# A transformer kernel's mixers: decays as products, level matmuls inside the projections, output projection begun early

## The chip, the cores and the metric

One core of one Trainium2 chip runs one program. The metric is the device time in microseconds. The kernel before took 1440.02 us (median of 3 runs, 1439.94 to 1443.43).

## The reference

Two transformer blocks on 256 positions of width 1024, in float32. The change lies in the first block's mixers:

```python
h = rms_norm(x, norm_mix); z = h @ w_in           # 9 splits: a_x a_y | b_q b_f b_i b_g | c_q c_k c_v
# LRU group (a_x, a_y; width 256)
xc = causal_conv4(a_x) + conv_b
r, i = sigmoid(xc @ wa + ba), sigmoid(xc @ wx + bx)      # 64x64 blocks
log_a = -8 * r * softplus(-lam); a = exp(log_a)
u = sqrt(-expm1(2 * log_a)) * (i * xc)
h_t = a_t * h_{t-1} + u_t;  ya = h * gelu(a_y)
# HGRN2 group (4 heads of 64)
log_f = log(lb + (1 - lb) * sigmoid(f)); k = (1 - lb) * sigmoid(-f); qs = silu(q)
# lb = cumsum(softmax(.)) - first = 0 for one layer: exp(log_f) = sigmoid(f) (+ tiny)
att[t, s] = sum_d q[t, d] * k[s, d] * exp(b[t, d] - b[s, d])   for s <= t,  b = cumsum(log_f)
yb = rms_norm(att @ v + carried state) * silu(g)
# attention group (8 heads of 64, causal with a linear bias; one block of 256, so no retrieval)
yc = softmax(q k^T / 8 - slope * distance) v
x = x + concat(rms_norm(ya), yb, rms_norm(yc)) @ w_out
# then MLP relu^2, the second block (gated linear attention, spatial gating, PEER), final norm
```

## The kernel before

Each product with a large weight matrix is done in three float32r matmuls: weights and activations are split into an upper and a lower part, and upper x upper, upper x lower and lower x upper are summed. The weights come as one stream of tiles of 128 x 1024 through a ring of four slots. Per tile, SyncE's queue loads `raw` (L310), ScalarE makes `whi` (`hi`, L511), GpSimd (POOL) `wlo` = raw - whi (`lo`, L406), and TensorE multiplies. ScalarE may fill a slot only when the tile four earlier has been used (`tile_used`).

There are two kinds of tiles. `f_tile` (L817 to L819) gives 128 output features by 256 positions from 24 matmuls of 256 columns; its result is in bank 4 or 5 in turn, and VectorE must copy it out (`in_f`) before the tile after next may start. `m_tile` (L834 to L836) adds one eighth of the contraction to four accumulators in banks 0 to 3, with 12 matmuls of 512 columns.

The order of each engine's work is written out by hand, one program per engine, tied by semaphores. The first block goes:

1. Squares, root and scaling of x, transposes (L864), upper and lower halves of the result (L541, L1203).
2. 16 f tiles: the features of a_x, a_y, q, f and the attention's q and k. VectorE copies them (L1270, L1272) and, after every second one, does an `ada_tile` (L1233, L1235), a piece of the second block's modulation vector: its weights have a second stream of 48 tiles, `ada`, with a ring of four slots of its own. `series` is a short polynomial in 2 columns for softplus(-lam).
3. 8 m tiles (values and gate, `zM`), with the LRU's gates (L888) before the fourth. Beside them VectorE makes the convolution (L1319, L1323), gelu's argument, log f by abs, exp and ln (L1335 to L1354), copies `zM` (L1351), and sums log f along time (L1361). ScalarE has the sigmoids (L570 to L580) and exp and ln (L587, L589).
4. The mixers. The scores of HGRN2 need the decay exp(b[t] - b[s]), which would overflow as exp(b[t]) times exp(-b[s]). The positions of each half of 128 are therefore paired at 7 levels with half-lengths h = 1 to 64: a query in the right half of a block of 2h and a key in the left half meet at the block's middle, with both factors at most one. For each level POOL subtracts (`level_diff`, L451), ScalarE takes exps (`level_dec`, L600, L601), POOL multiplies keys and queries into `hK` and `hQ` (`level_qk`, L462, L463), TensorE forms scores over all 128 x 128 pairs (`level_scores`, L966) and VectorE takes those of this level by a mask into `att` (`level_acc`, L1374). Level 0 is the diagonal, and an eighth step (L954) ties the two halves of 128. Between the levels stands one attention head each: `a_scores` (L914, L915), `a_soft` (L1386, L1389), `head_exp` (L609), `a_turn` (L924), `head_pT` (L1396), `a_values` (L933 to L935). The LRU's parts are at levels 3 and 5 (L1407 to L1417, with the scan in L1415). Then the LRU is transposed (L989), HGRN2's values are formed (L997, L1000), and the norms follow: squares (L526), POOL's root (L425, L427), scalings (L1446 to L1455).
5. y is transposed as a whole (L864, group `y_T`), split (L541, L1203), and 8 m tiles of `w_out` follow (group `wout`). After them come a modulation column group (`ada_columns`, L898) and the MLP's transposes (L864 with `xs`), then the MLP.

## Time and profile before

| | |
|---|---|
| runs | 1440.02 us median (1439.94 to 1443.43) |
| profiled execution | 1442.89 us, span 1441.1 us |
| busy: TensorE, VectorE, ScalarE, POOL | 1382.1, 769.4, 721.9, 1080.5 us |
| mean granted TensorE clock | 0.967 |
| first projection, f tiles; m tiles | 47.63; 25.76 us |
| mixers; output projection | 63.77; 23.80 us |

An engine's busy share says little by itself: TensorE is busy 96% of the span, and in the mixers it is busy too, but at half clock for much of it. The stretches of the first block are to be read apart, with the granted clock beside them. A row of the timeline has start and duration in us, engine, line, operation, operands, and in brackets the idle time before it and what ended it. Matmuls are pipelined: the distance between two starts is what a group costs.

### The profile page before, as it was taken

What the parts mean: (1) busy time and instruction counts of PE and PEld (TensorE: products, weight loads), DVE (VectorE), ACT (ScalarE), POOL (GpSimd) and SP (SyncE); (2) the same over time, 40 slices, a digit from 0 to 9 for tenths busy, and PEclk for the clock granted to TensorE, in tenths of its full rate; (3) what the DMA queues carried; (4) which work ended last, traced back from release to release, by engine and by line L of the source; (5) the groups of instructions that cost most, each with busy time, mean ns of one, the idle gap of its engine ahead of it and who ended that gap; (6) DMA issues with size and microseconds to landing.
All of it is one profiled execution on the core that took longest, in us unless ns stands there. A gap on an engine that the chain in (4) does not pass through costs nothing.

```text
span 1441.1 us, 29039 instructions
## 1 busy us (share of the span) xinstructions
PE 1382.1 (96%) x9746; PEld 1232.9 (86%) x9746; DVE 769.4 (53%) x1612; ACT 721.9 (50%) x1139; POOL 1080.5 (75%) x495
## 2 busy tenths in 40 slices
PE   6997899999899999899999999999999999999997
PEld 6976799999877787799999999999977777788885
DVE  3567433333518734519994156666678888611113
ACT  5364365555445454434556543344445555566664
POOL 7755578888569877686888877777767777788885
PEclk9986899999899999899999999999999999999999
DMA  9711467775444547654555554444444544475552
GB/s 343 282 45 60 156 216 284 274 289 196 176 148 161 171 136 261 205 182 133 188 178 186 179 171 160 159 156 157 155 146 162 172 161 162 161 259 190 190 197 94
DMA packets 72649, 262.99 MB, mean 182 GB/s; under 512 B 8208, under 2 KB 9104, under 8 KB 72224
## 3 DMA queue, kind: packets, MB, share of 16 engines
q1 hardware_dynamic: 72608, 262.46, 53.3%
q8 instruction: 23, 0.38, 0.1%
q14 instruction: 18, 0.15, 0.0%
HBM read 259.81 MB, written 2.62 MB: 182 GB/s over the span
## 4 chain that ended last, share of the span: by engine, by line
PE 85%; DVE 6%; issue 3%; POOL 2%; ACT 2%; DMA 1%; SPq 0%; POOLq 0%; ACTq 0%; DVEq 0%
PE bank L817 14%; PE bank L818 13%; PE bank L819 13%; PE bank L834 13%; PE bank L835 12%; PE bank L836 12%; PE bank L1132 3%; POOL wlo L406 2%; DVE arena L1563 1%; DMA raw<-stream 1%; PE bank L966 1%; DMA arena<-ada 1%; PE bank L898 1%; PE bank L1114 1%; PE bank L864 0%
## 5 line engine op out<-in xcount | busy, mean ns | idle before, releaser
L406 POOL TENSOR_TENSOR wlo<-raw,whi 128x1024 fp32r<-128x1024 f32 x432 | 1042.6, 2426 | 301.3 <-ACT whi L511 297.8
L511 ACT ACTIVATE whi<-raw 128x1024 fp32r<-128x1024 f32 x432 | 453.8, 1052 | 190.6 <-PE bank L836 99.4
L817 PE MATMUL bank<-xh,whi 128*128 128x256 f32 x1600 | 459.9, 287 | 6.9 <-DVE xl L1203 4.4
L818 PE MATMUL bank<-xl,whi 128*128 128x256 f32 x1600 | 453.9, 284 | 0.0
L819 PE MATMUL bank<-xh,wlo 128*128 128x256 f32 x1600 | 453.7, 284 | 0.0
L817 PEld LDWEIGHTS bank<-xh,whi 128*128 128x128 f32 x1600 | 308.3, 193 | 10.5 <-POOL wlo L406 5.0
L818 PEld LDWEIGHTS bank<-xl,whi 128*128 128x128 f32 x1600 | 308.4, 193 | 1.2
L819 PEld LDWEIGHTS bank<-xh,wlo 128*128 128x128 f32 x1600 | 308.1, 193 | 0.0
L834 PE MATMUL bank<-whi,uh 128*128 128x512 f32 x640 | 255.4, 399 | 2.3 <-DVE ul L1757 2.3
L835 PE MATMUL bank<-wlo,uh 128*128 128x512 f32 x640 | 250.4, 391 | 0.0
L836 PE MATMUL bank<-whi,ul 128*128 128x512 f32 x640 | 249.9, 390 | 0.0
L1757 DVE TENSOR_TENSOR ul<-bank,uh 128x256 fp32r<-128x256 f32 x128 | 54.4, 425 | 183.7 <-ACT bank L784 183.7
L836 PEld LDWEIGHTS bank<-whi,ul 128*128 128x128 f32 x640 | 120.5, 188 | 25.4
L834 PEld LDWEIGHTS bank<-whi,uh 128*128 128x128 f32 x640 | 120.8, 189 | 24.4 <-DVE ul L1757 2.4
L757 ACT ACTIVATE arena<-bank 128x256 f32 x128 | 49.3, 385 | 181.0 <-PE bank L819 180.8
L835 PEld LDWEIGHTS bank<-wlo,uh 128*128 128x128 f32 x640 | 120.8, 189 | 21.9
L783 ACT ACTIVATE uh<-arena 128x256 fp32r (+1 forms) x128 | 53.5, 418 | 164.0 <-PE bank L836 160.8
L1742 DVE TENSOR_TENSOR xs<-bank,xs 128x768 bf16<-128x768 f32 x128 | 121.7, 951 | 0.0
L834 PE MATMUL bank<-whi,xh 128*128 128x512 f32 x288 | 116.3, 404 | 5.2 <-POOL wlo L406 2.4
L835 PE MATMUL bank<-wlo,xh 128*128 128x512 f32 x288 | 114.3, 397 | 0.0
L836 PE MATMUL bank<-whi,xl 128*128 128x512 f32 x288 | 113.8, 395 | 0.0
L1750 DVE TENSOR_TENSOR arena<-arena,bank 128x256 f32 (+1 forms) x128 | 53.3, 416 | 67.3 <-PE bank L1132 67.3
(284 smaller groups left out, 1346.4 us busy)
## 6 DMA issues: line engine op xcount, KB each, us to landing
raw<-stream SPq DMA_DIRECT2D x432, 512.0 KB, 3.3
arena<-ada SPq DMA_DIRECT2D x48, 512.0 KB, 4.3
arena<-rows SPq DMA_DIRECT2D x5, 512.0 KB, 7.5
xs<-x SPq DMA_DIRECT2D x2, 512.0 KB, 4.4
arena<-rows SPq DMA_DIRECT2D x1, 1024.0 KB, 4.6
x_spill<-xs SPq DMA_DIRECT2D x1, 1024.0 KB, 6.2
xs<-x_spill SPq DMA_DIRECT2D x1, 1024.0 KB, 5.6
out<-arena SPq DMA_DIRECT2D x2, 512.0 KB, 2.6
```

What stands on the lines that cost most here:

```text
L406: nc.gpsimd.tensor_tensor(wlo[:, slot, :], raw[:, slot, :], whi[:, slot, :].bitcast(F32), ALU.subtract).then_inc(lo_done, 1)
L511: nc.scalar.activation(whi[:, slot, :], raw[:, slot, :], ACT.Copy).then_inc(hi_done, 1)
L783: nc.scalar.activation(uh[:, c % 2, :], src, ACT.Copy)
L817: nc.tensor.matmul(dst, h_, xh[:, k, :], start=(k == 0), stop=False)
L818: nc.tensor.matmul(dst, h_, xl[:, k, :], start=False, stop=False)
L819: last = nc.tensor.matmul(dst, l_, xh[:, k, :], start=False, stop=(k == KC - 1))
L834: nc.tensor.matmul(bank[b][:, :], ah[:, ts], whi[:, slot, cs], start=start, stop=False)
L835: nc.tensor.matmul(bank[b][:, :], ah[:, ts], wlo[:, slot, cs], start=False, stop=False)
L836: last = nc.tensor.matmul(bank[b][:, :], al[:, ts], whi[:, slot, cs], start=False, stop=final)
L1742: ttt(oneA[:, slot], same.unsqueeze(1).to_broadcast([P, 3, 4, HALF]), picks[:, 2:5, ts].unsqueeze(3).to_broadcast([P, 3, 4, HALF]), ALU.mu ...
L1750: ttt(dst, dst, bank[6 + q % 2][:, 0:4 * HALF].rearrange("p (t n) -> p n t", t=4), ALU.mult)\
L1757: ttt(ul[:, c % 2, :], bank[5][:, 0:T], uh[:, c % 2, :].bitcast(F32), ALU.subtract)\
```

## The change

It does the following.

- **Decays as products.** log f, its running sum, and the exps per level are gone. sigmoid(f) and 1 - sigmoid(f) come from one exp, an addition, a reciprocal and a product (q's sigmoid likewise, and f and q are first raised to at least -85). `totals(h)` multiplies neighbours, so that `tot(h)` (banks 6 and 7) holds the product of the decays over each run of h positions, with a copy in SBUF. From level to level `level_up(h)` multiplies the keys of each left half by the product of its right neighbour's run, and the queries of each right half by that of its left one, in place. `hQ`, `hK`, `hdec`, and all of POOL's and ScalarE's level work go.
- **Level matmuls between tiles.** `level_scores(0)` stands after f tile 13, 1 to 7 before m tiles 1 to 7, the cross-half one behind. Levels 6 and 7 form only the blocks that are used; levels 5 to 7 share banks and one masked copy.
- **LRU within the f tiles.** The f tiles are reordered (`F_ORDER`), so that a_x comes first, then f, q, a_y. Convolution, gates (after tile 4), decay, scan and gelu lie between the copies of the f tiles, with intermediate results in banks 0 to 3.
- **Modulation tiles.** The twelve `ada_tile`s of this part move from the f tiles (0 to 7) and the output projection (8 to 11) to levels 2 to 5 (0 to 3) and the output projection (4 to 11); their DMAs in SyncE's queue move along. Column group 1 is formed after the output projection.
- **Mixers.** Only the attention, the HGRN2 values and the norms are left. `head_pT` goes from VectorE to ScalarE, the next scores wait for the raw copy (`a_raw`) and not the minimum, silu(g) is made from tanh.
- **Output projection.** `y_turn(b)` transposes two of the eight column blocks of y at a time: LRU and HGRN2 blocks within heads 5 and 6, the attention's before m tile 3. The first tile takes banks 2, 3, 0, 1.

The diff, cut to its core:

```diff
@@ tables @@
+TOT_AT = {2: 0, 4: 256, 8: 384, 16: 448, 32: 480, 64: 496}
+F_ORDER = [0, 1, 6, 7, 4, 5, 2, 3, 8, 9, 10, 11, 12, 13, 14, 15]
+    if group == "wout":
+        return (("att_y", 1), ("att_y", 2), ("a_pT", 8), ("a_raw", 8))[bank]
...
+        def tot(h):
+            return bank[7][:, :] if h == 1 else bank[6][:, TOT_AT[h]:TOT_AT[h] + 512 // h]
@@ SyncE @@
+            for n in range(R, T_FFN):
+                tile(n % R, n * P, n - R + 1)
+                if n in range(T_IN_M, T_IN_M + R):
+                    ada_tile(n - T_IN_M)
+                if n in range(T_WOUT, T_WOUT + R):
+                    ada_tile(n - T_WOUT + R)
...
@@ POOL: level_diff and level_qk go @@
-            los(R, T_WOUT)
...
+            los(R, T_WOUT + R)
             root(S("squares"), squared("lru"), s_(SS["lru"]), rs("lru"), 1.0 / 256)
+            root(S("hg_ss"), 1, hss, hrs, 1.0 / 64)
             root(S("squares"), squared("att"), s_(SS["att"]), rs("att"), 1.0 / 512)
@@ ScalarE, f tiles @@
+            nc.scalar.activation(hk, zF[:, 6:8, :], ACT.Exp, scale=-1.0).then_inc(S("hk_exp"), 1)
+            upper_of(R + 4, R + 6)
             act.wait_ge(S("lru_gates"), 1)
...
+            upper_of(R + 6, R + 7)
+            act.wait_ge(S("in_f"), 6)
+            nc.scalar.activation(hq, zF[:, 4:6, :], ACT.Exp, scale=-1.0).then_inc(S("hq_exp"), 1)
...
@@ TensorE @@
+            def level_scores(n):
+                pe.wait_ge(S("h_qk"), n + 1)
...
+                first = 4 if n else 2
+                for odd in range(2):
+                    ps = slice(64 * odd, 64 * odd + 64)
+                    for c in range(2):
...
+                        h = P if n < 6 else LEVELS[n - 1]
+                        for tt in range(TT):
+                            dst, at = (2 * tt + c) * P, tt * P
+                            for a in range(0, P, 2 * h):
+                                ks = slice(at + a, at + a + h)
+                                qs = ks if h == P else slice(at + a + h, at + a + 2 * h)
...
+                                last = nc.tensor.matmul(bank[first + odd][a:a + h, to], hk[ps, c, ks], hq[ps, c, qs],
+                                                        start=True, stop=True)
+                    last.then_inc(S("h_sc"), 1)
...
+            m_group(T_IN_M, "in_M", before=lambda k: level_scores(k) if k else None)
+            level_scores(8)
...
+            for h in range(8):
+                a_turn(h)
+                if h + 2 < 8:
+                    a_scores(h + 2)
+                if h == 0:
+                    hg_values()
+                if h:
+                    a_values(h - 1)
+                if h >= 5 and h < 7:
+                    y_turn(h - 5)
+            a_values(7)
+            def att_turn(k):
+                if k == 3:
+                    y_turn(2)
+                    y_turn(3)
+            m_group(T_WOUT, "wout", "y", before=att_turn, first_banks=(2, 3, 0, 1))
@@ VectorE @@
+            def totals(h):
+                even_odd = lambda t_: t_.rearrange("p (a two) -> p a two", two=2)
+                src, copy_ = even_odd(tot(h)), even_odd(tot_copy(h))
+                for dst in (tot(2 * h), tot_copy(2 * h)):
+                    own(ttt(dst.unsqueeze(2), src[:, :, 0:1], copy_[:, :, 1:2], ALU.mult))
...
+            own(tsc(two(bank[1]), hq, 1.0, None, ALU.add)); own.sync()
+            own(nc.vector.reciprocal(bank[1][:, :], bank[1][:, :])); own.sync()
+            ttt(hq, two(bank[1]), zF[:, 4:6, :], ALU.mult).then_inc(S("h_qk"), 1)
...
+            def level_up(h):
...
+                own(ttt(k0, t2[:, :, 1:2].to_broadcast([P, 256 // h, h]), k0, ALU.mult))
+                ttt(q1, t2[:, :, 0:1].to_broadcast([P, 256 // h, h]), q1, ALU.mult).then_inc(S("h_qk"), 1)
...
+            for n in range(1, 8):
+                v.wait_ge(S("h_sc"), 2 * n + 2)
+                v.wait_ge(S("h_qk"), n + 1)
+                level_up(LEVELS[n - 1])
+                if n < 5 or n == 7:
+                    level_acc(n)
+                if 2 <= n < 2 + R:
+                    ada_tile(n - 2)
```

What moves, at three places. First TensorE. Before, behind the last m tile of the first projection (L836), a head's scores, two modulation column groups and the levels (L966) begin:

```order
L836 MATMUL bank<-whi,xl 128x512
L914 MATMUL bank<-arena 128x128 [waits in_m]
L915 MATMUL bank<-arena 128x256
L898 MATMUL bank<-st,arena 128x1 [waits ada_used,ones_set]
L898 MATMUL bank<-st,arena 128x1 x3
L966 MATMUL bank<-arena 128x128 [waits ri_done,hb_done]
L966 MATMUL bank<-arena 128x128 x7
L914 MATMUL bank<-arena 128x128 [waits a_max]
```

Now level 7 (L899) stands between two of those m tiles (L826 to L828), and only the cross-half step (L889) is behind them, ahead of the first scores (L935):

```order
L828 MATMUL bank<-whi,xl 128x512
L899 MATMUL bank<-arena 64x64 [waits h_qk]
L899 MATMUL bank<-arena 64x64 x7
L826 MATMUL bank<-whi,xh 128x512 [waits lo_done]
...
L889 MATMUL bank<-arena 128x128 [waits h_acc,h_qk]
L889 MATMUL bank<-arena 128x128 x3
L935 MATMUL bank<-arena 128x128 [waits in_m]
L936 MATMUL bank<-arena 128x256
```

The eight matmuls of a level have moved in front of a tile, and they wait for `h_qk`, which VectorE gives.

Second VectorE within the f tiles. Before, between the copies of tiles 11 and 12 (L1272, L1270), a modulation tile (L1235, `arena` the weights) and the polynomial in 2 columns:

```order
L1272 TENSOR_SCALAR arena<-bank 128x256 [waits tile_used] x2
L1235 SCALAR_TENSOR_TENSOR bank<-arena,st,bank 128x512 [waits ada_used,ada_full1]
L1235 SCALAR_TENSOR_TENSOR bank<-arena,st,bank 128x512 [waits dve_steps]
L1295 TENSOR_TENSOR bank<-bank,arena 128x2
```

Now, between the copies of tiles 7 (L1285) and 8 (L1283), q's sigmoid, and behind tile 8's the first products of decays (L1324):

```order
L1285 COPY arena<-bank 128x256 [waits tile_used]
L1366 TENSOR_SCALAR bank<-arena 128x512 [waits xc_done,hq_exp]
L1367 RECIPROCAL bank<-bank 128x512 [waits dve_steps]
L1368 TENSOR_TENSOR arena<-bank,arena 128x512 [waits dve_steps]
L1283 TENSOR_SCALAR arena<-bank 128x256 [waits tile_used]
L1324 TENSOR_TENSOR bank<-bank,arena 128x256
```

The copy of tile 8 now stands behind a wait for ScalarE's exp and a reciprocal, and tile 10 waits for that copy.

Third TensorE at the start of the output projection. Before, the last value products of HGRN2 (L997, L1000), then all of y's transposes (L864) and the first m tile:

```order
L997 MATMUL bank<-arena 128x64
L1000 MATMUL bank<-arena 128x64
L864 MATMUL bank<-ident,arena 128x128 [waits unturned]
L864 MATMUL bank<-ident,arena 128x128 x7
L834 MATMUL bank<-whi,xh 128x512 [waits turned_lo,lo_done]
```

Now the second y turn (L987), the last head's turn (L945) and the values of the last two heads (L954 to L956) stand right before it:

```order
L987 MATMUL bank<-ident,arena 128x128 [waits y_ready]
L987 MATMUL bank<-ident,arena 128x128 x3
L945 MATMUL bank<-ident,arena 128x128 [waits a_pT,a_exp]
L945 MATMUL bank<-ident,arena 128x128 x2
L954 MATMUL bank<-arena 128x64 [waits a_pT]
L955 MATMUL bank<-arena 128x64
L956 MATMUL bank<-arena 128x64
L826 MATMUL bank<-whi,xh 128x512 [waits a_pT,lo_done,turned_lo]
```

The first m tile no longer waits for a transpose of the whole y, only for its first two blocks.

## Rows read from the trace of the kernel before

**Rows 1.** Stretches: length, busy time (instructions) by engine, granted clock, DMA share, GB/s.
```profile
14.65:62.28 47.63, 47.63 (x384) 47.63 (x385) 22.80 (x58) 20.02 (x23) 38.73 (x17) 0.96 0.85 315
62.28:88.04 25.76, 24.31 (x114) 18.93 (x112) 19.07 (x29) 16.86 (x21) 12.87 (x6) 1.00 0.49 168
88.04:151.81 63.77, 48.40 (x302) 41.58 (x301) 44.97 (x82) 28.89 (x75) 34.86 (x34) 0.63 0.10 34
151.81:175.61 23.80, 23.80 (x99) 19.56 (x99) 10.15 (x17) 8.57 (x11) 15.93 (x7) 0.92 0.50 176
```
**Rows 2.** Timeline of ScalarE, one upper half in each kind of tile.
```profile
48.08 1.06 ACT L511 ACTIVATE whi<-raw 128x1024 fp32r<-128x1024 f32 x1 [1.82 <-PE bank L819]
...
162.04 1.06 ACT L511 ACTIVATE whi<-raw 128x1024 fp32r<-128x1024 f32 x1 [1.66 <-PE bank L836]
```
**Rows 3.** Waits, 100 to 180: us in total, times, longest.
```profile
DVE xs L1465 <- PE bank L836: 13.2, 1, 13.2
...
PE bank L966 <- DVE arena L1374: 7.6, 2, 5.1
...
PE bank L864 <- DVE arena L1455: 6.3, 1, 6.3
```
**Rows 4.** Stretches as in rows 1, within the mixers and at the output projection's start.
```profile
90.80:104.20 13.40, 13.40 (x79) 11.42 (x79) 7.15 (x17) 7.57 (x24) 10.06 (x11) 0.50 0.00 1
104.20:111.85 7.65, 7.65 (x71) 6.08 (x70) 7.37 (x15) 3.80 (x11) 6.75 (x8) 0.99 0.01 2
...
128.49:141.20 12.71, 12.68 (x67) 11.71 (x67) 6.68 (x14) 7.04 (x16) 6.81 (x6) 0.50 0.26 88
147.47:155.30 7.83, 7.17 (x24) 6.10 (x25) 4.83 (x11) 3.03 (x8) 0.00 (x0) 0.50 0.00 0
```
**Rows 5.** Timeline of TensorE: gates, one head at half clock, one level at full.
```profile
72.08 1.95 PE L888 MATMUL bank<-arena 64*64 64x256 f32 x16 [1.45 <-DVE arena L1323]
...
98.48 0.63 PE L914 MATMUL bank<-arena 64*128 64x128 f32 x2
...
99.89 0.69 PE L933 MATMUL bank<-arena 128*128 128x64 f32 x2
...
101.22 0.85 PE L924 MATMUL bank<-ident,arena 128*128 128x128 f32 x3
102.00 2.08 PE L966 MATMUL bank<-arena 64*128 64x128 f32 x16
...
105.99 1.16 PE L966 MATMUL bank<-arena 64*128 64x128 f32 x16
106.99 0.38 PE L914 MATMUL bank<-arena 64*128 64x128 f32 x2
107.21 0.59 PE L915 MATMUL bank<-arena 64*128 64x256 f32 x2
```
**Rows 6.** VectorE's groups by form, 26 to 62: busy, mean ns, idle before.
```profile
L1235 DVE SCALAR_TENSOR_TENSOR bank<-arena,st,bank 128x512 f32<-128x512 f32 x10 | 7.5, 751 | 0.2
```
**Rows 7.** Timeline of VectorE and of POOL.
```profile
82.86 2.76 DVE L1343 SCALAR_TENSOR_TENSOR arena<-arena 128x512 f32<-128x512 f32 x1
...
120.85 5.52 DVE L1415 TENSOR_TENSOR_SCAN arena<-arena 128x256 f32<-128x256 f32 x2
...
82.66 2.41 POOL L406 TENSOR_TENSOR wlo<-raw,whi 128x1024 fp32r<-128x1024 f32 x1 [2.44 <-ACT whi L511]
```
**Rows 8.** VectorE's groups by form, 0 to 182.
```profile
L1374 DVE COPY_PREDICATED arena<-arena,bank 128x512 f32<-128x512 uint32 x14 | 9.4, 731 | 4.0 <-PE bank L966 4.0
...
L1424 DVE RECIPROCAL arena<-arena 128x16 f32<-128x16 f32 x1 | 0.2, 243 | 0.0
L1301 DVE RECIPROCAL bank<-bank 128x2 f32<-128x2 f32 x1 | 0.2, 179 | 0.0
```
**Rows 9.** ScalarE's groups by form, 0 to 182.
```profile
L600 ACT ACT_TABLE_LOAD x2 | 2.6, 1283 | 0.0
```
**Rows 10.** The chain that ended last, one column group.
```profile
175.61 0.79 PE bank L898 x8
```

More of the change, by code:

```diff
@@ L1339, in _ @@
[L1339 to L1348 removed]
+            tsc(c8, acc, -8.0, None, ALU.mult).then_inc(S("c8_done"), 1)
```

588 lines of the change are left out of this document (288 added, 300 removed).

## The prediction

> **What bounds the kernel now.** I read the table of the stretches first [rows 1]. TensorE is the engine that fills nearly all of the span, so a stage is worth what TensorE spends in it. The first projection's 16 tiles (14.65 to 62.28) keep it busy all of 47.6 us; its other 8 tiles (62.28 to 88.04) take 25.8; the mixers (88.04 to 151.81) take 63.8, with TensorE busy for 48.4 of them at a mean granted clock of 0.63; the output projection takes 23.8. After 175.61 the change touches only modulation work, so its whole effect is by how much that point moves.
>
> Two periods are the metronomes [rows 2]. A tile of the first kind (24 matmuls of 256 columns) takes 2.88 us: ScalarE's upper half, 1.06, after a wait of 1.82 for the tile's end. One of the second kind (12 matmuls of 512) takes 1.06 + 1.66 = 2.72; eight make 21.8.
>
> Then the waits of the mixers [rows 3]: TensorE waits 6.3 us for the last scaling of y and 7.6 for masked copies. Last the clock [rows 4]: TensorE is busy 13.4 of 13.4 us at half clock (1.2 GHz) from 90.80, at full from 104.20, and busy 12.7 of 12.7 at half again from 128.49. The start of the output projection (151.81 on) is at half too.
>
> **First projection, 16 tiles.** TensorE gets two inserts. The LRU's gates move in from the next stage, 1.95 us at 72.08 [rows 5]. The level-0 scores are 8 matmuls of 64 rows by 128 columns, in the trace two records each. At full clock 16 such records took 1.0 us (105.99 to 106.99), but there the two row halves alternate; now all of one half come first (the loop over `odd` is outermost). The nearest rows without alternation are an attention score's: 2 records of 128 columns in 0.22 us (106.99 to 107.21) [rows 5], so 16 x 0.11 = 1.7 or 1.8. Bounds 1.0 and 1.8; I take 1.7, as the order is that of the scores. Sum 47.6 + 1.9 + 1.7: the stage ends at 65.9.
>
> Does VectorE keep up? Tile n+2 may start only when tile n is copied out. Between copies VectorE now does, instead of modulation scalings (two of 0.75 us per pair of tiles) [rows 6], the convolution, two sigmoids made from exp, add, reciprocal and product, 12 products of decays of 256 down to 8 columns, and the LRU with its scan. POOL's subtractions are no obstacle: the scalings, with one input in SBUF and one in PSUM, keep 0.75 beside them [rows 6], while L1343 with both inputs in SBUF took 2.76 when POOL had begun one of 2.41 just before it, at 82.66, and the two scans 5.5 together [rows 7]. The moved steps have a PSUM side, but for one of 2 columns.
>
> The unknown is the reciprocal over 512 columns, twice. The rows have 0.179 us for 2 columns and 0.243 for 16 [rows 8]: 4.6 ns a column, 2.5 us for 512; the masked copy, an ordinary pass over 512, takes 0.73 [rows 8]. Ends 0.7 and, with the ratio doubled since two small rows bear little, 5.0; I take 3.0. The tight place is the second one. Tile n ends at 27.9 + 2.88(n-3), from tile 5 on 1.9 later. ScalarE turns tile 9's upper half when tile 5 ends (35.6), then a table load (1.28 [rows 9]), four gate sigmoids (some 0.4 each), an upper, a load and the exp of q: 42.3. VectorE: 0.7 + 3.0 + 0.7, then tile 8's copy (0.4): 47.1. Tile 10 wants that at 47.1 (end of tile 9). So no stall at 3.0 us, and one us for each us more.
>
> The Trainium skill, "VectorE: DVE Perf Modes", section "First, the fixed hardware budget", says that reciprocal is an iterative divide with a repeat count of 8. Read as 8 cycles for each column at the 0.96 GHz that the page gives, this is an estimate of 4.3 us and a stall of 1.3; the row of 16 columns lies below such a slope, and the sum by the page would be 1.3 us worse.
>
> **Second kind, 8 tiles.** 21.8 us, plus levels 1 to 5 at 1.7 (8.5); level 6 as 16 matmuls of 32 columns, 32 records (between 0.9, by their columns, and 3.2 at the 0.1 per record of the one-column matmuls, 0.79 for 8 [rows 10]; I take 1.7); level 7 with half the columns (1.0); the cross-chunk one, 4 matmuls (0.8); and 0.1 per switch (0.6). That is 34.4 us instead of 25.8: +8.6, end at 100.3. VectorE has per level two products of 256 columns (0.8), two masked copies (1.5) and a modulation tile (1.5): 3.8 against TensorE's 4.4, so hidden. The masked copies kept their time beside POOL's small steps; if they wait for its 2.4 us subtractions in six levels, up to +10, which I hold unlikely and price at nothing.
>
> **Mixers.** VectorE finishes level 7 at 98.8 and copies four banks (4 x 0.68): 101.5. TensorE idles 1.2 us, then has the attention before it, I assume at half clock: 8 pairs of scores at 1.41 (98.48 to 99.89), 11.3; 8 value products at 1.33 (to 101.22), 10.6; 8 turns at 0.78 (to 102.00), 6.2 [rows 5]; the HG values, 24 records of a value product's kind (1.33 for 6), 5.3; LRU turn and two y turns, 4 transposes each, 1.0 apiece; one column group 1.4. Sum 37.8, and 0.3 before the first output tile; less 1.3, since the clock fell only at 90.8, 2.8 us after the dense tiles' end (88.04) [rows 1, 4]. The other engines are under TensorE's 3.5 us per head: in the 13.4 us stretch, with three heads and three levels, VectorE was busy 7.2 and ScalarE 7.6 [rows 4]; ScalarE gets one copy of 384 columns per head more and loses the decays. So the first output tile starts at 101.5 + 36.8 = 138.3; the stage takes 38.0 instead of 63.8: -25.8. What disappears with the levels is the tail after the HG values (root, scaling, 16 transposes, first split, the 6.3 us wait of [rows 3] in it), now beside the heads.
>
> **Output projection.** Tile 0 begins with banks 2 and 3 while VectorE divides the attention out of 0 and 1. The attention rows are needed at tile 4; squares, root and scaling of them are part of today's tail, 10.6 us as a whole (141.2, where the stretch of [rows 4] ends, to 151.81). Against it stand three tiles, 8.2 us; at worst 2.4 is seen, I take none. Two y turns are inserted, 8 transposes at full clock, 1.0. The cold start stays (23.8 - 21.8 = 2.0). One more column group follows, 0.8 [rows 10]. So 25.6, +1.8. VectorE's eight modulation tiles, 12 us, and their DMAs fall in a stage in which it idled 13.2 in one piece [rows 3].
>
> **Sum.** +3.6 + 8.6 - 25.8 + 1.8 = -11.8 us. The profiled execution took 1442.9 (span 1441.1), so 1431.1 for it; the median of the runs, 1440.0, lies 2.9 under it: 1428.2, said as 1428.
>
> **Rivals.**
> (a) The clock is released within the attention, as at 104.20 today. For: TensorE now works there without gaps. Against: the same mix of heads and HG values from 128.49 stayed at half for 12.7 busy us [rows 4]. Released after 13.4 us of work, the remaining 24 us halve, but are then bound by the other engines (about 2.4 us a head, 14 in all): -10; and the output projection starts warm, -1.8: 1416. The Trainium skill, "TensorE: Matmul & The Clock Gate", section "What's actually happening", has "the default state is throttled, and activity releases the throttle"; by that alone this would be the forecast. The 13.4 busy us at half show that the busy time of such small matmuls does not suffice.
> (b) VectorE can't feed the first projection: a reciprocal of 4 to 5 us and slower passes on PSUM stall TensorE at several tiles, some 6 us in all: 1434. For: each copy now queues behind up to 4.9 us of work. Against: the average between copies stays under 2.4.
> (c) Slower than before: level matmuls between the dense tiles drop the clock to half in the second stage. They are 12.6 of its 34.4 us, of a kind seen at half while busy [rows 4]. The dense part then adds up to 21.8, the levels up to 12: 1428 + 34 = 1462; it decides from 12 us of loss on, about a third of the stage at half. Against: the gates amid the same tiles today cost no clock, even with 1.45 us idle ahead [rows 5].
> (d) The overlap isn't had: a wait inside the heads puts the engines in series, and the mixers keep 50 us: 1440. Every wait in the loop is fed one head ahead, which speaks against it.
>
> **How the numbers follow.** Forecast 0.60, (a) 0.22, (b) 0.11, (c) 0.05, (d) 0.02. The likeliest case's own range is 1422 to 1434: levels at 1.0 (-4), level 6 (-1, +1.5), reciprocal (+2), late attention rows (+2.4), small gaps in the heads (+2). The 8-in-10 range goes down into (a), to 1415, and up over (b), to 1435. A change under 0.3%, 4.3 us, can hardly be told from none here: faster 0.92, same 0.03, slower 0.05.
>
> **What would show it.** Right: level scores of 1.7 us between 512-column matmuls, a first output tile near 138, the MLP's transposes near 164, a granted clock of 0.50 from about 103 into the first output tiles. Clock 1.0 and a head period near 2.4 us mean (a); 256-column matmuls waiting for copies out of PSUM mean (b); a clock under 0.8 between 66 and 100 us means (c). Wrong: mixers over 45 us with gaps in TensorE.

## The result and the profile after

The changed kernel takes 1428.76 us (median of 5 runs, 1427.28 to 1433.12); beside it on the same chip the kernel before took 1440.05 (median of 5, 1439.94 to 1444.59). The ratio is 0.9914, with a 95% interval of 0.9900 to 0.9928: faster by 0.7 to 1.0%. The prediction was 1428.

The profiled execution took 1428.76 us, its span is 1426.9 and its mean granted clock 0.978. The span is 14.2 us shorter than that of before (1441.1), more than the 11.3 of the medians, because the profiled execution of before lies 2.9 above its median, and this one lies on it.

The stretches of the changed kernel, answering to [rows 1]: first projection's 16 tiles, its other 8 with the levels between, the mixers, the output projection with its column groups up to the MLP's transposes. The columns are the stretch, its length, busy time and instructions of PE, PEld, DVE, ACT and POOL, the granted clock and the DMA share with its GB/s.
```profile
15.25:68.45 53.20, 52.54 (x417) 51.10 (x418) 36.89 (x88) 31.78 (x42) 38.93 (x17) 1.00 0.64 221
68.45:102.20 33.75, 33.75 (x233) 26.64 (x231) 19.20 (x36) 8.94 (x9) 20.03 (x9) 1.00 0.55 187
102.20:138.60 36.40, 35.14 (x150) 27.88 (x149) 17.53 (x42) 15.81 (x51) 5.10 (x5) 0.58 0.09 29
138.60:163.07 24.47, 24.47 (x123) 20.64 (x122) 18.35 (x28) 11.28 (x16) 17.91 (x10) 1.00 0.73 257
```
The first two stages got longer (53.2 for 47.6, 33.8 for 25.8), the mixers far shorter (36.4 for 63.8), with TensorE busy 97% of them, and that at 0.58 of its clock. Behind the output projection the column groups begin at 161.37 where it was 175.44 by the timeline, 14.1 us earlier; as one group more costs 0.9, the MLP's transposes come 13.2 earlier (163.07 for 176.25), and the program ends 14.2 earlier: 1.0 comes back behind them, at no single place.

TensorE's timeline in the changed kernel: starts, busy time, line and shapes; a bracket is idle time before it, and what ended it. The first row is level 0; then levels 6 and 7 and the cross-half scores; the first attention score; two rows of a head with the next head's first; the first `y_turn`, and the MLP's transposes.
```profile
60.88 1.71 PE L899 MATMUL bank<-arena 64*128 64x128 f32 x16
...
94.20 0.60 PE L899 MATMUL bank<-arena 64*32 64x32 f32 x32
97.70 0.96 PE L899 MATMUL bank<-arena 64*64 64x64 f32 x16
101.56 0.72 PE L889 MATMUL bank<-arena 64*128 64x128 f32 x8
103.17 0.48 PE L935 MATMUL bank<-arena 64*128 64x128 f32 x2 [0.89 <-DVE arena L1435]
...
122.01 0.85 PE L945 MATMUL bank<-ident,arena 128*128 128x128 f32 x3
122.79 0.79 PE L935 MATMUL bank<-arena 64*128 64x128 f32 x2
125.70 0.85 PE L945 MATMUL bank<-ident,arena 128*128 128x128 f32 x3
...
133.07 1.06 PE L987 MATMUL bank<-ident,arena 128*128 128x128 f32 x4
...
163.07 1.94 PE L856 MATMUL bank<-ident,xs 128*128 128x128 f32 x16
```
A head at half clock takes 125.70 - 122.01 = 3.69 us, with no bracket in it: TensorE alone sets it. The granted clock in the stretches that the clock's course needs:
```profile
100.00:105.00 5.00, 4.11 (x29) 3.02 (x28) 4.62 (x11) 2.89 (x3) 3.55 (x2) 1.00 0.43 154
105.00:106.00 1.00, 1.00 (x7) 0.83 (x7) 0.33 (x2) 0.72 (x4) 0.21 (x1) 0.77 0.00 0
105.50:136.20 30.70, 30.70 (x117) 24.16 (x117) 13.75 (x32) 11.90 (x45) 2.74 (x4) 0.50 0.06 18
136.00:137.00 1.00, 1.00 (x10) 0.99 (x9) 0.00 (x0) 0.61 (x2) 0.00 (x0) 0.87 0.00 0
```
Full clock (2.4 GHz) to 105.5, half (1.2 GHz) to about 136.2 with TensorE busy all the time, full again before the first output tile at 138.60. The rise falls in the second `y_turn` (135.74). In the kernel before the output projection began at half [rows 4].

### The profile page after: what moved, and what is told of

Its sections match the earlier page's. It is cut to its first block, busy times and chain, and to the rows that moved or that the text cites. A ratio compares the mean times of both kernels' runs of the same rounds, so it can differ in the third digit from the quotient of the medians.

```text
span 1426.9 us, 29009 instructions
## 1 busy us (share of the span) xinstructions
PE 1380.6 (97%) x9762; PEld 1228.5 (86%) x9762; DVE 763.6 (54%) x1620; ACT 714.1 (50%) x1128; POOL 1056.3 (74%) x469
## 4 chain that ended last, share of the span: by engine, by line
PE 41%; POOL 30%; issue 21%; DVE 4%; DMA 2%; ACT 1%; POOLq 1%; SPq 0%; ACTq 0%; DVEq 0%
POOL wlo L426 30%; PE bank L826 8%; PE bank L827 8%; PE bank L828 8%; PE bank L809 4%; PE bank L811 4%; PE bank L810 4%; DMA raw<-stream 2%; DVE arena L1613 1%; PE bank L899 1%; PE bank L919 0%; PE bank L936 0%; PE bank L935 0%; DMA arena<-ada 0%; POOLq L425 0%
## 5 line engine op out<-in xcount | busy, mean ns | idle before, releaser
L826 PE MATMUL bank<-whi,uh 128*128 128x512 f32 x640 | 255.0, 398 | 3.0 <-DVE ul L1807 3.0
L828 PE MATMUL bank<-whi,ul 128*128 128x512 f32 x640 | 249.2, 389 | 0.0
L826 PEld LDWEIGHTS bank<-whi,uh 128*128 128x128 f32 x640 | 120.5, 188 | 25.5 <-DVE ul L1807 2.4
L828 PEld LDWEIGHTS bank<-whi,ul 128*128 128x128 f32 x640 | 120.1, 188 | 25.5
L826 PE MATMUL bank<-whi,xh 128*128 128x512 f32 x288 | 115.9, 403 | 4.1 <-DVE arena L1585 2.0
L828 PE MATMUL bank<-whi,xl 128*128 128x512 f32 x288 | 113.2, 393 | 0.0
```

Source lines behind the costliest of these rows:

```text
L826: nc.tensor.matmul(bank[b][:, :], ah[:, ts], whi[:, slot, cs], start=start, stop=False)
L828: last = nc.tensor.matmul(bank[b][:, :], al[:, ts], whi[:, slot, cs], start=False, stop=final)
```

## The experiments

All are edits of the changed kernel. Each was timed beside the kernel before on its own chip (medians there 1441.59 for the first four, 1442.55 for the next four, 1440.47 for three, 1441.03 for the last), so the ratio to before is the better comparison between runs; the changed kernel's is 0.9914. Where the text names the kernel's mean clock, it is TensorE's granted clock over the whole span.

None of these edits reaches behind the MLP's transposes, and yet the profiles take from 1262.9 to 1267.9 us from there to the end. The clock drops at a few places there, in the changed kernel's profile at about 350 and 580 us above all, and for differing lengths in the profiles. So part of every difference of whole times is of that kind, and beside the median stands, where it helps, when the MLP's transposes begin in the profile: 163.07 in the changed kernel.

### Row halves in turn

```diff
-                for odd in range(2):
-                    for c in range(2):
-                        for tt in range(TT):
-                            for a in range(0, P, 2 * h): matmul(...)
+                for c, tt, a in blocks:
+                    for odd in range(2): matmul(...)
```


> The level matmuls take the two row halves in turn (odd innermost), as the kernel before did; nothing else changes. Theory (my price of 1.7 us for a level is the order's): each of levels 0 to 5 falls from 1.64 to about 1.0 us (16 records at the 1.0 us that the kernel before showed at 105.99), the cross-chunk one by 0.3; as TensorE is the bound there, the kernel gets 3.5 to 4.3 us faster than the changed kernel (1428.8 to about 1425). Rival: the level matmuls wait for something else, or VectorE then bounds the stage (its work per level is 3.8 us against a tile and a level of 2.72 + 1.0 = 3.7): the level is shorter in the profile, but the time stays within 1 us.

1424.59 us (1422.78 to 1426.53), ratio 0.9883, interval 0.9862 to 0.9903: 4.2 us under the changed kernel by the medians, 4.4 by the ratios. TensorE's groups by form, levels 1 to 5 (five levels of 16 records), first of the changed kernel:
```profile
L899 PE MATMUL bank<-arena 64*128 64x128 f32 x80 | 8.5, 284 | 0.0
```
and then with the halves in turn:
```profile
L898 PE MATMUL bank<-arena 64*128 64x128 f32 x80 | 5.8, 284 | 0.0
```
A level went from 1.70 to 1.16 us, 0.54 less; six such levels make 3.2, and the two of smaller blocks another 0.4 (0.96 to 0.68, 0.60 to 0.46). The MLP's transposes come 4.0 us earlier (159.06). So the price of 1.7 us that the prediction took from the order of the loops was right, its lower bound of 1.0 was nearly to be had for nothing (1.09 from start to start), and VectorE doesn't bound the stage. The rival falls. One expected part is missing: the cross-half scores, changed in the same way, were to gain 0.3 and took 0.71 where they took 0.72:
```profile
97.50 0.71 PE L891 MATMUL bank<-arena 64*128 64x128 f32 x8
```
I can't explain that. As each row half writes a bank of its own, the edit also makes the banks alternate; which of the two counts was not tested.

### Levels behind the tiles instead of between

```diff
-            m_group(T_IN_M, "in_M", before=lambda k: level_scores(k) if k else None)
-            level_scores(8)
+            m_group(T_IN_M, "in_M")
+            for n in range(1, 9):
+                level_scores(n)
```


> The eight tiles of the second kind run without inserts; levels 1 to 8 follow as a block of their own behind them; VectorE's program is unchanged. Theory (the levels gain by lying between tiles, since each needs VectorE's products and copies of the one before): TensorE's stage is 11.8 us shorter, but a level then lasts as long as VectorE's part, 0.8 + 1.5 + 1.5 us = 3.8 and a few tenths of handovers, eight times 4 = 30 us; net +14 to +20 us. Rival (they gain nothing by it, VectorE ran ahead already in the tiles): net under +3 us. The granted clock should fall to 0.5 within the block of levels, as it does in the heads.

1449.88 us (1447.35 to 1452.09), ratio 1.0058, interval 1.0038 to 1.0077: 21 us slower than the changed kernel, and slower than the one before. TensorE's timeline in it:
```profile
89.34 1.71 PE L899 MATMUL bank<-arena 64*128 64x128 f32 x16
93.22 2.65 PE L899 MATMUL bank<-arena 64*128 64x128 f32 x16 [2.18 <-DVE arena L1408]
98.05 3.06 PE L899 MATMUL bank<-arena 64*128 64x128 f32 x16 [2.17 <-DVE arena L1408]
```
The first level, still at full clock, lasts 3.9 us: 1.7 of matmuls and a wait of 2.18 for VectorE's products and masked copies. The third (98.05) and those like it last 5.2, since the matmuls take 3.07 at half clock. Between tiles that wait lies under 2.72 us of dense work, and the clock stays full. The theory holds. I had put a level at 4 as VectorE's part alone; in fact its products and copies stand in series with TensorE's matmuls, and only the modulation tile lies beside them. The whole block took 30.3 us (89.34 to 119.59), as expected, because the last three steps are shorter. What goes beyond the expected 14 to 20 us comes behind the block: the first attention score is 17.5 us later than in the changed kernel (120.63 for 103.17), the MLP's transposes 21.9, and the clock stays at half from the heads into the output projection, to about 162.

### Output projection not begun early

```diff
-                if h >= 5 and h < 7:
-                    y_turn(h - 5)
             a_values(7)
...
-            m_group(T_WOUT, "wout", "y", before=att_turn, first_banks=(2, 3, 0, 1))
+            for b in range(4):
+                y_turn(b)                 # each waits for the whole of y
+            m_group(T_WOUT, "wout", "y")
```
ScalarE's and VectorE's halves of y move behind the attention's scaling in the same way.

> The output projection no longer begins with the LRU's and HG's rows: all 16 transposes of y stand behind the last head and wait for the whole of y, and its first tile begins behind them; the rest of the change stays. Theory (the tail of the attention was a term of its own, today's 10.6 us between 141.20 and 151.81 in the kernel before): the first output tile comes 8 to 12 us later, the two inserted transposes of 0.8 and half of the heads' 2.0 go, and the kernel is 7 to 11 us slower than the changed one (about 1437). Rival (the late rows would be hidden anyway, the gain is all from the levels): under 3 us.

1438.59 us (1435.8 to 1440.74), ratio 0.9977, interval 0.9965 to 0.9989: 9.8 us slower than the changed kernel by the medians, 9.1 by the ratios. TensorE's timeline in it:
```profile
137.58 0.64 PE L951 MATMUL bank<-arena 128*128 128x64 f32 x2
142.41 3.68 PE L980 MATMUL bank<-ident,arena 128*128 128x128 f32 x16 [4.20 <-DVE arena L1487]
145.74 0.78 PE L821 MATMUL bank<-whi,xh 128*128 128x512 f32 x1
```
A wait of 4.20 us for squares, root and scaling, and 3.3 us of transposes at half clock: 7.5 us between the last head and the first output tile, and the first output matmuls are at half clock (0.63 each up to 147.16) where the changed kernel's are at full. The MLP's transposes come 7.1 us later (170.13); the rest of the difference lies behind them. Without the early beginning the kernel is 0.2% under the one before. This and the levels' place are no shares of one sum: each alone can undo most of the gain or more.

### Unread dense matmuls in the heads

```diff
+            def fill(count):              # 128 rows x 512 columns, float32r, result unread
+                pe.wait_ge(lo_done, T_WOUT + 1)
+                for _ in range(count):
+                    nc.tensor.matmul(bank[6], whi[:, 0, 0:P], xh[:, 6:8, :], start=True, stop=True)
+            fill(4)                       # behind the cross-chunk scores
             for h in range(8):
                 a_turn(h)
+                fill(4)
```


> Adds matmuls whose result nobody reads (128 rows, 512 columns, the type of the projection's): 4 behind the cross-chunk scores and 4 in each of the 8 heads, 36 in all, 0.23 us each at full clock and 0.43 at half. Theory (wide dense matmuls hold the clock that small ones lose; the 3.69 us per head is the price of the half clock): granted clock 1.00 through the heads, a head at 1.85 + 0.9 = 2.7 us instead of 3.7, the kernel 5 to 8 us faster than the changed one. Rival 1 (the clock depends on the busy share alone, and that is near 100% already): clock stays 0.5, 36 x 0.43 = 15 us slower. Rival 2 (clock full, but the other engines bound a head at about 3.5): no change within 2 us.

1421.51 us (1419.14 to 1424.24), ratio 0.9866, interval 0.9840 to 0.9891: 7.3 us faster for 36 matmuls of needless work. TensorE's timeline, one head:
```profile
117.12 0.50 PE L953 MATMUL bank<-ident,arena 128*128 128x128 f32 x3
117.38 1.17 PE L918 MATMUL bank<-xh,whi 128*128 128x512 f32 x4
118.48 0.48 PE L943 MATMUL bank<-arena 64*128 64x128 f32 x2
...
120.05 0.50 PE L953 MATMUL bank<-ident,arena 128*128 128x128 f32 x3
```
A head takes 2.93 us at a clock of 1.00. Both rivals fall. Which of the fills did it is open: those ahead of the heads or those within.

### Dense fill ahead of the heads only

```diff
             fill(4)                       # behind the cross-chunk scores
             for h in range(8):
                 a_turn(h)
-                fill(4)
```


> Only the 4 unread dense matmuls behind the cross-chunk scores, none in the heads: they fill TensorE's 0.89 us of idle time ahead of the first attention score. Theory (the clock is lost in the heads, to the kind of their work, not to that gap): clock at 0.5 from about 105 us as in the changed kernel, no change within 1.5 us. Rival (the idle gap makes the clock fall, and once up it would stay): clock 1.00 through the heads without fills, heads at 2.0 to 2.4 us, -10 us.

My theory was wrong. 1420.11 us (1418.69 to 1425.46), ratio 0.9858, interval 0.9833 to 0.9883: 1.1 us of dense work ahead of the heads, in time that was idle for most of it, does all of it. The stretch with the heads:
```profile
105.00:125.00 20.00, 18.10 (x125) 14.04 (x124) 13.64 (x33) 12.60 (x47) 2.74 (x4) 1.00 0.09 27
```
The clock stays at 1.00 through 20 us of heads in which nothing is dense and TensorE even idles 1.9 us. So the small matmuls don't drop the clock by themselves: in every profile with half clock in the heads it was lost at their beginning, and in the four profiles that had it full there it stayed full. The first output tile comes at 126.41 instead of 138.60, the MLP's transposes at 150.91, 12.2 us earlier; 1.7 of them are lost again where the clock drops near 340. These rows are from the second head to the fourth (L953 is the turn, as L945 above):
```profile
112.53 0.50 PE L953 MATMUL bank<-ident,arena 128*128 128x128 f32 x3
113.48 0.46 PE L943 MATMUL bank<-arena 64*128 64x128 f32 x2 [0.45 <-DVE arena L1458]
...
115.52 0.52 PE L953 MATMUL bank<-ident,arena 128*128 128x128 f32 x3 [0.34 <-ACT arena L599]
...
117.54 0.50 PE L953 MATMUL bank<-ident,arena 128*128 128x128 f32 x3
```
A head takes 2.0 to 3.0 us, and waits for VectorE and ScalarE appear in it: the other engines bound it now.

### What the filler must be: idle time, density, or both

Three kernels take this apart. The first fills the gap of 0.89 us with useful narrow work that stood behind it:
```diff
-            pe.wait_ge(S("in_m"), 4)
-            a_scores(0)
             pe.wait_ge(S("ones_set"), 1)
             ada_columns(0)
+            pe.wait_ge(S("in_m"), 4)
+            a_scores(0)
```


> The first modulation column group (4 pairs of one-column matmuls, 0.9 us) stands ahead of the first attention score, in TensorE's 0.89 us of idle time, instead of behind it; no work is added. Theory A (that idle time is what drops the clock to half at 104.8): clock 1.00 through the heads, heads at 2.2 us, about 1418 to 1420. Theory B (the four dense matmuls held the clock by their own work, filling a gap with one-column matmuls doesn't): clock 0.5 as before, only the 0.9 us of the group itself is saved, 1428. In between, some executions at 1418 and others at 1428: the decision is close to its edge.

1427.96 us (1427.32 to 1433.25), ratio 0.9912, interval 0.9894 to 0.9930; the mean clock is 0.972 to 0.978 in all six. As theory B has it (the MLP's transposes come 0.9 us earlier, at 162.14), with one flaw: the gap wasn't closed but moved, to 105.2.
```profile
101.70 1.05 PE L919 MATMUL bank<-st,arena 128*128 128x1 f32 x8
...
105.91 0.90 PE L945 MATMUL bank<-ident,arena 128*128 128x128 f32 x3 [0.74 <-ACT arena L590]
```

The second keeps the dense fill and opens the gap again:
```diff
+            for _ in range(2):            # VectorE, ahead of the copies of zM
+                own(nc.vector.tensor_copy(h2f, bank[7][:, :])); own.sync()
```


> The 4 unread dense matmuls behind the cross-chunk scores stay, but VectorE makes two extra copies of 512 columns (0.68 us each) ahead of its four copies of the second half's result, so that TensorE idles about 1.3 us again ahead of the first attention score. Theory A (the idle time drops the clock): clock 0.5 in the heads, 1430 (1428.8 and the 1.3). Theory B (four more dense matmuls hold it whatever the gap): 1421.5.

1431.3 us (1430.39 to 1434.79), ratio 0.9935, interval 0.9914 to 0.9956. The dense fill is there, and the clock falls:
```profile
101.64 1.19 PE L918 MATMUL bank<-xh,whi 128*128 128x512 f32 x4
104.06 0.48 PE L943 MATMUL bank<-arena 64*128 64x128 f32 x2 [1.22 <-DVE arena L1447]
...
104.91 1.85 PE L927 MATMUL bank<-st,arena 128*128 128x1 f32 x8
```
The column group, 1.05 us at full clock, takes 1.85 from 104.91 on. The MLP's transposes come 2.4 us later than in the changed kernel (165.48). Theory A by itself would explain this. Two things go with it: the gap is wider than the 0.89 that it stands for, and VectorE has two copies more.

The third mends the flaw of the first: the same filler time as the dense one, at the same place, with everything behind it in place.
```diff
...
+            for j in range(4):            # one-column matmuls, 8 records, result unread
+                nc.tensor.matmul(bank[6][:, j:j + 1], ada_sum(0)[:, j * P:(j + 1) * P], one, start=True, stop=True)
             pe.wait_ge(S("in_m"), 4)
             a_scores(0)
```


> The same gap ahead of the first attention score as in the changed kernel, filled with 4 unread one-column matmuls (8 records, 0.95 us) in place of 4 dense ones (0.94 us); everything behind them starts at the same time as in the run with the dense fill at the start only, so that run differs from this one by the kind of the filler alone. Theory B (the filler must be dense): the clock falls near 105 us, heads at 3.7 us, 1429 (the column group isn't saved here, the filler is extra but lies in idle time). Theory A (only the idle time mattered; moving the column group there had opened a new gap of 0.74 us at 105.2): clock 1.00, 1420.

1429.71 us (1427.49 to 1430.19), ratio 0.9918, interval 0.9900 to 0.9936. TensorE's timeline and a stretch:
```profile
101.33 1.05 PE L994 MATMUL bank<-st,arena 128*128 128x1 f32 x8
102.31 0.48 PE L935 MATMUL bank<-arena 64*128 64x128 f32 x2
103.16 1.48 PE L919 MATMUL bank<-st,arena 128*128 128x1 f32 x8
```
```profile
100.00:105.00 5.00, 5.00 (x35) 4.14 (x34) 4.07 (x9) 3.47 (x6) 2.89 (x2) 0.86 0.32 105
```
TensorE is busy 5.00 of 5.00 us, without any gap, and the clock falls before 105. So closing the gap (this run) or dense work with a gap behind it (the run before) didn't keep the clock in any of their ten executions; both together did. The three kernels with dense work and no gap (fills in the heads too, at the start only, and the last version below) have a mean clock of 0.981 or more in 12 of 13 executions; the thirteenth, 1425.46 us at 0.979, lies between. Of the 54 executions of the changed kernel and of its other edits, but for the one with the levels behind the tiles, 50 are at 0.979 or less. The other four, of two kernels that leave a gap (below), are at 0.985 to 0.987. So dense work without a gap shifts the odds strongly; it is no condition without which the clock can't be kept, and what decides in a single execution isn't shown.

The moment of the fall isn't tied to one instruction either: in the seven profiles of edits or of the changed kernel that have the levels between the tiles, `y_turn`s within the heads and half clock there, it lies 2.9 to 5.0 us behind the start of the cross-half scores (3.98 in the changed kernel, 2.93 in this run).

### Three edits together, with two and with one dense matmul per head

The halves in turn; the second reciprocal in two halves of 256 columns with tile 8's copy between them:
```diff
-            own(nc.vector.reciprocal(bank[1][:, :], bank[1][:, :])); own.sync()
+            own(nc.vector.reciprocal(bank[1][:, 0:T], bank[1][:, 0:T]))
+            in_f(8)
+            own(nc.vector.reciprocal(bank[1][:, T:2 * T], bank[1][:, T:2 * T])); own.sync()
             ttt(hq, two(bank[1]), zF[:, 4:6, :], ALU.mult).then_inc(S("h_qk"), 1)
-            in_f(8)
```
and `fill(2)` ahead of the heads, with `fill(2)` or `fill(1)` in each.

> Three edits together on the changed kernel: the row halves of the level matmuls in turn (-4.2 us as measured), the second reciprocal in two halves with tile 8's copy between them (the stall of 0.66 us goes), and 2 unread dense matmuls ahead of the heads and 2 in each head instead of 4. Theory (two hold the clock as well as four, and at full clock TensorE still sets a head's length): clock 1.00, a head at 2.93 - 0.47 = 2.5 us, the stage 4.2 us shorter than with four: 1421.5 - 4.2 - 0.7 - 4.2 = 1412. Rival 1 (two don't hold the clock): heads at 3.7 + 0.9 = 4.6 us, 1432. Rival 2 (ScalarE or VectorE bound the head at 2.9): 1416.

> As the run with three edits, but 1 unread dense matmul in each head. Theory (there is an amount of dense work below which the clock falls, and one of 0.23 us in 2.2 us is below it): clock about 0.5 in the heads, a head at 3.7 + 0.43 = 4.1, the kernel at 1428 or above. Rival 1 (one holds the clock too, TensorE sets the head at 2.2 to 2.3): 1410. Rival 2 (one holds the clock, but ScalarE and VectorE bound the head at 2.4): as with two, 1412.

With two: median 1430.52, but the six runs fall in two groups, 1415.87 and 1417.77 at a mean clock of 0.986, and four of 1430.19 to 1434.12 at 0.972 to 0.975. The profiled one is of the first group and shows heads at 2.5 us (111.80 to 114.28; 2.53 the one before), as the theory has it, though not its 1412 us; the other four, not profiled, fit Rival 1 by time and mean clock. With one: 1428.22 (1426.41 to 1430.67), all six at 0.978 or less, heads of 4.1 us in the profile. In both kernels two fills left a gap, here in the profile of the first:
```profile
98.04 0.74 PE L918 MATMUL bank<-xh,whi 128*128 128x512 f32 x2
99.05 0.49 PE L943 MATMUL bank<-arena 64*128 64x128 f32 x2 [0.27 <-DVE arena L1446]
```
That the number per head is what differs would be the wrong reading. In the second kernel the clock falls at about 101.6, ahead of the first head's fill (L918, the last row):
```profile
101.32 0.74 PE L944 MATMUL bank<-arena 64*128 64x256 f32 x2
101.99 0.90 PE L953 MATMUL bank<-ident,arena 128*128 128x128 f32 x3
102.54 0.78 PE L918 MATMUL bank<-xh,whi 128*128 128x512 f32 x1
```
Up to there the two kernels are the same, and in the two profiles TensorE's groups from the cross-half scores to L944 stand at the same distances within 0.02 us; one kept the clock and one lost it. So whether one dense matmul per head would hold a clock that is up wasn't tested, and something that these rows don't show decides near the edge. The median of such a kernel says little; its executions have to be read one by one, with their clock.

### The version that beats both

Halves in turn, split reciprocal, `fill(6)` ahead of the heads and none in them.

> Row halves in turn, the second reciprocal in two halves, and 6 unread dense matmuls ahead of the heads, none in them. With the halves in turn TensorE is through sooner and its wait for VectorE is the same 0.95 us, so that 4 would fill it and 6 (1.4 us) leave none. Theory A (no idle time, no fall): clock 1.00 through the heads in every execution, 1420.1 - 4.2 - 0.7 + 0.5 = about 1416. Theory B (the shorter level matmuls also thin the work ahead of the heads): some executions fall and take 1428.

1415.56 us (1414.67 to 1419.69), ratio 0.9831, interval 0.9812 to 0.9850: 1.7% under the kernel before and, by the ratios, 0.8% under the changed one. All five runs have a mean clock of 0.981 to 0.988. Its MLP transposes begin at 145.90, 17.2 us earlier than in the changed kernel, of which 13.2 are left at the end of the span: 1.7 go near 340 us and most of the rest between 530 and 590, where the clock drops for longer in this execution. Theory A holds. In this profile the gap is gone:
```profile
95.80 0.71 PE L891 MATMUL bank<-arena 64*128 64x128 f32 x8
96.44 1.66 PE L918 MATMUL bank<-xh,whi 128*128 128x512 f32 x6
98.04 0.48 PE L943 MATMUL bank<-arena 64*128 64x128 f32 x2
```

### The price of a reciprocal in the tight place

```diff
+            own(nc.vector.reciprocal(h2f, bank[1][:, :]))      # result overwritten later
             own(nc.vector.reciprocal(bank[1][:, :], bank[1][:, :])); own.sync()
```


> Before the second reciprocal over 512 columns VectorE makes it once more, into a buffer that is overwritten later; all else is the changed kernel. Theory (the prediction's: the copy of tile 8 is the tight place, and each us more there is one us of stall): the wait of tile 10 grows from 0.66 us by 3.4 to 4.0, the first stage ends 3.4 us later, and the kernel takes 1432 instead of 1428.8. Rival 1 (VectorE has slack there and the 0.66 is from something else): under 1 us more. Rival 2 (VectorE is late again at several later tiles): 5 us more or above.

1433.99 us (six runs). Four are 1433.82 to 1435.96 at a mean clock of 0.972 to 0.975, 5 to 7 us over the changed kernel, or 4 to 6 by the ratios; two are 1421.07 and 1421.76 at 0.987. The profile is of the four. First VectorE's row in the changed kernel, with TensorE's wait for the copy behind it:
```profile
44.70 3.37 DVE L1367 RECIPROCAL bank<-bank 128x512 f32<-128x512 f32 x1
...
49.18 0.38 PE L809 MATMUL bank<-xh,whi 128*128 128x256 f32 x1 [0.66 <-DVE arena L1283]
```
and then with the doubled one:
```profile
43.43 3.36 DVE L1367 RECIPROCAL arena<-bank 128x512 f32<-128x512 f32 x1
46.70 3.30 DVE L1368 RECIPROCAL bank<-bank 128x512 f32<-128x512 f32 x1
...
51.12 0.58 PE L809 MATMUL bank<-xh,whi 128*128 128x256 f32 x1 [3.87 <-DVE arena L1283]
```
3.27 us more on VectorE made 3.21 more of stall and no second one: one for one, as the prediction had it. But the stall also cost the clock, which the prediction didn't have. It falls within the wait, at about 49.2, and comes back at about 56.0, after 4.9 us of dense matmuls:
```profile
50.00:56.00 6.00, 4.88 (x23) 4.88 (x24) 5.11 (x12) 3.46 (x4) 2.38 (x1) 0.50 0.47 183
```
From the wait's end to 56.0 TensorE's matmuls fall 2.2 us further behind those of the changed kernel, so 3.3 us more on VectorE cost 5.4. (The profile began its tiles 1.3 us earlier by chance, and level 0 comes 4.1 us later, at 64.98.) The size is Rival 2's, but it comes from the clock and not from later waits. The two quicker runs I can't explain: by their mean clock they may have kept it in the heads, with no edit near there. No profile was taken of them.

## Why the prediction was right

The forecast, 1428, with the half clock through the heads, came true. Its terms, by its own steps:

- **First projection, 16 tiles**: said to end at 65.9, ended at 68.45. Gates 1.9 (31.99 to 33.87) and level 0 1.64 were as said. The reciprocal took 3.37 us where 3.0 was taken, 6.6 ns a column where the small rows gave 4.6, and the exp before it ended 0.3 later than reckoned from the first tile's start; together that is a stall of 0.66 (0.9 with the restart of the matmuls) instead of none. By the page of the Trainium skill that the prediction named ("VectorE: DVE Perf Modes", section "First, the fixed hardware budget"), read as eight cycles a column, it would have been 4.3; it measured 3.37. Gates and level 0 cost 0.3 more than their own time in restarts. The rest, 1.3 us, is the start: the first tile begins at 15.25 against 14.65, and its matmuls stand 0.21 us apart, the distance at half clock, until 20.1, where in the profile of before they do so from 15.6 to 19.0. (The view of the granted clock says 1.00 there for the changed kernel, which doesn't fit its matmuls; that stays open.) Over all profiles here that start lies between 14.56 and 15.39, so it is an execution's chance, not the change.
- **Second kind**: +8.6 said, +8.0 measured (33.75). Levels 1 to 5 were 1.64 each from start to the next tile, and 0.25 apiece for the switches where 0.1 was taken; level 6 took 0.60 where 1.7 was taken: the range's lower end, 0.9, by its columns, was still too high. Rival (c), a clock lost between level matmuls, is refuted by a granted 1.00 in the whole stage. The levels' worth there was also shown from the other side: behind the tiles they cost 21 us.
- **Mixers**: -25.8 said, -27.4 measured. The heads came at 3.69 us (3.5 said), the HG values took 5.2 (5.3), TensorE waited 0.89 ahead of the first score (1.2). The stage gained on the estimate mostly because the clock rose again at about 136.2, in the last heads; the prediction had it at half to the end and into the output projection. That it fell late, at about 105.5, was nearly in the sum (2.8 us taken behind the dense tiles, about 3.3 measured). Why it rose there isn't shown. In the same seven profiles as above the rise lies 0.3 to 2.3 us behind the start of the second `y_turn`, and without these turns in the heads it came only at 147.4, in the first output tile.
- **Output projection**: first tile at 138.60 (138.3 said). From there the MLP's transposes come 24.5 us later. The 25.6 said has only the added column group in it, so 26.4 answers to that: 1.9 less. The cold start of 2.0 that I kept went with the clock's early return, the column groups took 1.7 together, and no late attention row was seen.
- **Sum**: the parts were off by +2.6, -0.6, -1.6 and -1.9 us, 1.5 us in all: the MLP's transposes come 13.2 us earlier and the end 14.2, where 11.8 was said. For a profiled execution the prediction said 1431.1, and this one took 1428.8. The median moved by 11.3, since the profiled execution of before lay 2.9 us above its median and this one doesn't. So the hit to a microsecond is luck in part: the sum was off by 2.4 us at the end, and the distance of the two profiles from their medians gave that back.

Rival (a), the clock released in the heads, had 0.22 and 1416. It didn't happen in any of the five runs of the changed kernel, by their mean clocks (0.971 to 0.979), but it was nearer than I said: a kernel that differs by 1.1 us of dense work in idle time does it in three or four runs of four (1420.1), and one that differs by a reciprocal far off seems to have done it in two of six. The rule of the Trainium skill, "TensorE: Matmul & The Clock Gate", section "What's actually happening" ("activity releases the throttle"), which the prediction set against the row at half clock, doesn't decide here: 30.7 us of TensorE at 100% busy passed before it rose, 20 us at 91% didn't drop it. What was wrong in my reasoning was to take the clock as a property of the heads' work. The forecast of half clock came true, but what set it was the passage into the heads. Rival (b) is refuted but for its 0.66 us, and rival (d) by the head period without a bracket in it.

## What to carry to other kernels

When a serial chain of small matmuls runs between two engines (a level, products and masked copies, the next level), put its links between dense tiles of the same engine: here a link cost 1.6 to 1.9 us there, and as a block of its own 3.9 at full clock and 5.2 at half. Where a dense stage is followed by small matmuls, look at what stands directly ahead of them: an idle gap there went with half clock for the whole stage behind it in nearly all executions here, and unread dense matmuls in the gap are a cheap test of that. Read the executions one by one, with their clock, since near the edge those of one kernel differ by up to 18 us. When VectorE stalls a dense stage for some microseconds, count the clock with the stall. Try the two row halves in turn for matmuls of 64 rows: most groups gained by it here, one didn't.

## What the runs showed of the hardware

- The same small matmuls ran 20 us at full clock, or stood 30.7 us at half with TensorE busy throughout. Four 512-column matmuls ahead of them (1.1 us) without a gap behind went with the full clock, the same number of one-column matmuls (1.0 us) without a gap didn't, and dense ones with 1.22 us idle behind didn't. Four executions of other kernels kept the clock, by their mean, with a gap there.
- A wait of 3.87 us between dense tiles took the clock to half, and 4.9 us of dense matmuls passed before it was back. The 0.66 us wait of the changed kernel at the same place cost no clock.
- Eight matmuls of 64 rows by 128 columns (16 records) take 1.16 us with the row halves (and banks) in turn and 1.70 one half after the other. Four of them (8 records) take 0.71 and 0.72. With 32-column blocks, 32 records take 0.46 and 0.60 us.
- A reciprocal over 512 columns takes 3.30 to 3.37 us with PSUM on both sides, 3.36 into SBUF, and 1.77 over 256: 6.4 to 6.9 ns a column.
- Masked copies of 512 columns took 1.38 us for two beside GpSimd's subtractions of 2.4, and 1.31 in the block of levels, where GpSimd was idle; no stall of TensorE is put down to them.
- Two scans over 256 columns took 5.52 us in the kernel before, with all operands in SBUF [rows 7] and GpSimd's subtractions beside them (5.04 us from 120.80), and 1.27 in the changed one, with an input and the result in PSUM. Which of the two made the difference was not tested.
